# Turning the attention probabilities of a prompt in 64-query halves instead of 128-query tiles

## The reference, cut to what matters

```python
s_w = jnp.einsum('bqgpd,bwgd->bqgpw', qg, kw) - slope * d_w
p_w = masked_softmax(s_w, m_w)
o_w = jnp.einsum('bqgpw,bwgd->bqgpd', p_w, vw)
...
o = g[..., 0:1] * o_c + g[..., 1:2] * o_s + g[..., 2:3] * o_w
```

## Time and profile before

| | |
|---|---|
| median of 3 runs | 1911.8 us |
| lowest and highest | 1909.61, 1912.58 us |
| profiled execution: its span, first to last instruction | 1903.0 us (the page gives no other time of this execution) |
| TensorE matmuls busy | 1792.6 us, 94% |
| TensorE weight loads busy | 1441.7 us, 76% |
| VectorE busy | 672.6 us, 35% |
| ScalarE busy | 512.3 us, 27% |
| GpSimd busy | 100.0 us, 5% |
| chain that ended last | TensorE 47%, issue 8%, VectorE 5%, ScalarE 1% |
| prompt attention | from about 1310 to 1470 us |

### The profile page before, as it was taken

The page is one execution under the profiler, slowest core; times in us unless marked ns, Lnnn a source line. Parts: engine busy times, 40 slices in busy tenths (PEclk is TensorE's granted clock), DMA queues, the critical chain, the costliest instruction groups (busy, mean ns, idle before and its releaser), DMA issues.

```text
span 1903.0 us, 52710 instructions
## 1 busy us (share of the span) xinstructions
PE 1792.6 (94%) x23279; PEld 1441.7 (76%) x23279; DVE 672.6 (35%) x1804; ACT 512.3 (27%) x1216; POOL 100.0 (5%) x155
## 2 busy tenths in 40 slices
PE   6999999999898898999998999899999989999997
PEld 4876777777777577899987854687777778999985
DVE  6140226677664333111103400406887241111104
ACT  3112223333332122111112300315888131111103
POOL 2111100000000002000002000000000001000002
PEclk9999999999999898999999999999999998999998
DMA  8665835434434497999978992543000387999944
GB/s 308 213 213 193 269 115 169 119 111 123 120 108 146 130 274 270 387 409 415 418 314 252 223 220 90 169 111 103 2 2 2 77 346 268 411 413 417 417 179 169
DMA packets 195382, 413.48 MB, mean 217 GB/s; under 512 B 53686, under 2 KB 135314, under 8 KB 186674
## 3 DMA queue, kind: packets, MB, share of 16 engines
q1 hardware_dynamic: 176386, 357.95, 54.9%
q0 software_dynamic: 11040, 39.85, 5.8%
q10 hardware_dynamic: 7760, 12.79, 1.9%
HBM read 356.84 MB, written 57.91 MB: 218 GB/s over the span
## 4 chain that ended last, share of the span: by engine, by line
PE 47%; issue 8%; DVE 5%; ACT 1%; DVEq 1%; ACTq 0%
PE bank L2009 12%; PE bank L2004 6%; PE bank L2022 5%; PE bank L2028 4%; PE bank L1731 3%; PE bank L2888 3%; PE bank L2109 2%; PE bank L1986 1%; PE bank L1997 1%; PE bank L2998 1%; PE bank L3033 1%; DVE region_a L3299 1%; PE bank L2945 1%; PE bank L2820 1%; DVEq L3321 1%
## 5 line engine op out<-in xcount | busy, mean ns | idle before, releaser
L2004 PE MATMUL bank<-wg,slot_x 128*32 128x384 f32 x1056 | 123.0, 504 | 4.0 <-ACT slot_x L2198 2.7
L2009 PE MATMUL bank<-wg,slot_x 128*32 128x128 f32 x1056 | 124.4, 280 | 0.0
L2004 PE MATMUL bank<-wu,slot_x 128*32 128x384 f32 x1056 | 119.0, 486 | 3.7 <-issue 3.7
L2009 PE MATMUL bank<-wu,slot_x 128*32 128x128 f32 x1056 | 119.2, 273 | 0.0
L2022 PE MATMUL bank<-wd,actT 128*32 128x384 f32 x1056 | 117.5, 486 | 1.4 <-ACT actT L2221 1.4
L2028 PE MATMUL bank<-wd,actT 128*32 128x256 f32 (+1 forms) x704 | 118.1, 326 | 0.0
L2009 PEld LDWEIGHTS bank<-wg,slot_x 128*32 128x32 f32 x1056 | 116.7, 113 | 1.2
L2009 PEld LDWEIGHTS bank<-wu,slot_x 128*32 128x32 f32 x1056 | 115.2, 110 | 2.3
L639 PE MATMUL bank<-xm,wp 128*128 128x272 f32 x480 | 113.3, 395 | 0.0
L639 PEld LDWEIGHTS bank<-xm,wp 128*128 128x128 f32 x480 | 90.2, 190 | 20.7 <-issue 2.7
L2434 DVE TENSOR_TENSOR act<-bank,act 128x384 f32<-128x384 f32 x32 | 17.9, 558 | 249.0 <-PE bank L2009 249.0
(11 more groups left out here) (649 smaller groups left out, 4033.5 us busy)
## 6 DMA issues: line engine op xcount, KB each, us to landing
wg<-in_moe_w_gate_dram SPq DMA_DIRECT2D x22, 2048.0 KB, 11.6
wu<-in_moe_w_up_dram SPq DMA_DIRECT2D x22, 2048.0 KB, 16.3
wd<-in_moe_w_down_dram SPq DMA_DIRECT2D x22, 2048.0 KB, 11.6
xT<-in_ada_w_dram SPq DMA_DIRECT2D x40, 1024.0 KB, 5.5
w<-in_moe_w_gate_dram SPq DMA_DIRECT2D x10, 2048.0 KB, 11.6
fT<-in_moe_w_up_dram SPq DMA_DIRECT2D x10, 2048.0 KB, 16.2
gall<-in_moe_w_down_dram SPq DMA_DIRECT2D x10, 2048.0 KB, 11.3
wp<-in_rwkv_w_rkv_dram SPq DMA_DIRECT2D x24, 512.0 KB, 4.7
```

What stands on the lines that cost most here:

```text
L2004: mm = pe.matmul(ps[32 * j:32 * j + 32, 0:GW], x[:, k, 32 * j:32 * j + 32], w[:, k, 0:GW], start=k == 0, stop=k == KT - 1)
L2009: mm = pe.matmul(ps[96:128, q * 128:(q + 1) * 128], x[:, kk, 32 * q:32 * q + 32], w[:, kk, GW:FF], start=kk == 0, stop=kk == KT - 1)
```

## The change

The turn of a prompt unit is done in halves of 64 queries. For each head and key tile there are two transposes, one from partitions 0 to 63 and one from partitions 64 to 127, each against the matching quarter of the identity, with 64 moving columns. Half r of both heads goes to bank 4 + r. The waits for the two copies of the unit before are drawn together into one wait ahead of all transposes. pt_tr is posted by the last transpose of each half. ScalarE still makes two copies a unit, now one for each half with both heads, written to pieces of 64 columns of PT. The sample units' turn is as it was. PT's contents are the same.

```diff
--- before.py
+++ after.py
@@ -2991,12 +2991,15 @@
         if u >= NU:
             return sample_turn(u)
         j, i, br = UNITS[u]
+        if u >= 1:
+            pe.wait_ge(S("pt_ev"), 2 * u)
         for h in range(2):
-            if u >= 1:
-                pe.wait_ge(S("pt_ev"), 2 * u - 1 + h)
             for kt in range(i + 1):
-                mm = pe.transpose(bank[4 + h][:, kt * 128:(kt + 1) * 128], B.sc[u % NSC][:, h, kt * 128:(kt + 1) * 128], ident[:])
-            mm.then_inc(S("pt_tr"), 1)
+                at = (h * (i + 1) + kt) * 64
+                for r in range(2):
+                    mm = pe.transpose(bank[4 + r][:, at:at + 64], B.sc[u % NSC][hs(r), h, kt * 128:(kt + 1) * 128], ident[hs(r), hs(r)])
+                    if (h, kt) == (1, i):
+                        mm.then_inc(S("pt_tr"), 1)
 
     def sample_values(u):
         bq, gp = SUNITS[u - NU]
@@ -3130,11 +3133,13 @@
             j, i, br = UNITS[u] if u < NU else (None, None, None)
             if u >= NPT:
                 act.wait_ge(S("pv_mm"), u - NPT + 1)
-            for h in range(2):
-                n = i + 1 if u < NU else 4 - h
-                act.wait_ge(S("pt_tr"), 2 * u + h + 1)
-                act.activation(B.PT[u % NPT][:, h, 0:n], bank[4 + h][:, 0:128 * n].rearrange("p (k t) -> p k t", t=128), ACT.Copy)\
-                   .then_inc(S("pt_ev"), 1)
+            for r in range(2):
+                act.wait_ge(S("pt_tr"), 2 * u + r + 1)
+                if u < NU:
+                    dst, src = B.PT[u % NPT][:, :, 0:i + 1, r * 64:r * 64 + 64], bank[4 + r][:, 0:128 * (i + 1)].rearrange("p (h k t) -> p h k t", h=2, t=64)
+                else:
+                    dst, src = B.PT[u % NPT][:, r, 0:4 - r], bank[4 + r][:, 0:128 * (4 - r)].rearrange("p (k t) -> p k t", t=128)
+                act.activation(dst, src, ACT.Copy).then_inc(S("pt_ev"), 1)
             if (i, br) == (0, 0):
                 act.wait_ge(S("ptc_tr"), j + 1)
                 act.activation(B.PTc[j % 2], bank[6], ACT.Copy).then_inc(S("ptc_ev"), 1)
```

## The result

| | before | after |
|---|---|---|
| median (6 runs each) | 1910.7 us (1903.31 to 1915.73) | 1892.56 us (1888.32 to 1898.82) |
| ratio | | 0.9916, 95% interval 0.9893 to 0.9939 |
| span of the profiled execution | 1903.0 | 1890.1 |
| attention: first scores (line 2945) to the first matmul of the output projection (line 1731) | 183.61 | 177.51 |
| from there to the end | 415.52 | 408.87 |

The change makes the kernel faster by 18.1 us by these medians; later repetitions of both kernels put it at about 12. Forecast was 6.7. The attention gives 6.1 of the profiled difference of 12.9; 6.7 lie behind it and 0.15 ahead of it, where the change touches nothing.

A forecast was written before the change was run, and what follows sets the result against it. TensorE and VectorE were taken to share the bound in the prompt attention. Seven waits shortened by 0.79 (5.5 us) plus 1.2 at its end made 6.7 off 1911.8: 1905.1 us, range 1900.0 to 1914.0.

The forecast's parts named there:

- The bound: Prompt attention: TensorE and VectorE share the bound; VectorE's seven waits for scores shrink from 1.41 to 0.62 us each.
- behind the last compressed turn: End of the attention, after VectorE's last wait: TensorE sets the time, and shorter turns and passages save 1.2 us.
- the passage from turn to values: Prompt attention, last transpose to first values: 0.20 us instead of 0.11; the change of shape, 0.09, stays.
- The pairs side by side: Prompt turns: two half-height transposes run together, 0.06 us a pair, saving 0.05 of each 0.11.
- loads set the pace: Prompt turns: weight loads take 0.11 us a pair, so turns save nothing; 1910.6 us, chance 0.06.
- The second rival: Prompt turns: halves follow each other, with the relief of shape; 1915.0 us, chance 0.09.
- the passage from turn to scores: Prompt attention: the shared shape removes the 0.09 us change of shape and the exposed load, 0.20 together.
- The slower case: Prompt turns: halves follow each other and transposes don't share the scores' configuration, no passage gets cheaper; 1916.7 us, chance 0.10.
- the wait vanishes: Prompt attention: copies report sooner or the queue fills better, so the full 9.9 + 1.5 us go; 1900.4 us, chance 0.05.
- all later work moves with it: Behind the attention: output weights load when the values are done, so later work moves by the same 6.7 us.
- part on costs: Prompt attention on TensorE: 0.11 us a transpose step, 0.16 for the first, 0.09 for a change of shape.
- The base: Whole kernel: 6.7 us taken off the runs' median 1911.8, which lies 8.8 above the span of 1903.0.

The follow-up runs named there:

- The two kernels with the halves in turn: Kernel after, all transposes of queries 0 to 63 before those of 64 to 127: with a wait per half 0.9972, with one wait 1905.9 us.
- the single wait: Kernel after with all of half 0 transposed before half 1, and one wait for both copies ahead of all transposes: 1905.9 us.
- The shape break: Kernel after plus one full-shape (128*128), one-column matmul between the second turn of each pair of units and the scores: 1900.1 us.
- another order: Kernel after with second turn and following scores ahead of the second values once a head pair, ScalarE's store at its step's end: 0.9934 and 0.9948.
- the padding: 64 tiny transposes (128 TensorE instructions, results unused) ahead of the second layer's output projection: added to the kernel before 0.9997, to the kernel after 0.9966.

## Why the prediction was right in the attention and wrong in the time

**The bound was right.** VectorE's waits for the scores went from seven of 1.41 to eight of at most 0.62 and their sum to 4.4, "at 4 us in all" as predicted. From the second compressed turn on the attention gained 6.7 where 6.7 was summed, and 1.2 of it behind the last compressed turn as summed; a head pair gained 0.88 (one of the six 1.11) where 0.79 was summed. The starts of the turns hit to 0.05 us. That the values came at 0.64 and not 0.69 is the passage from turn to values: the prediction kept its 0.20 whole, but its 0.09 for the change of shape now come on top of 0.06 a pair, 0.15 in all.

**The pairs side by side** were priced rightly (0.06 a pair, 0.062 measured). The rival that loads set the pace at 0.11 is refuted by it. The Trainium skill's rule (TensorE: Matmul & The Clock Gate, "LDWEIGHTS") would give 0.11 too (an estimate, 128 columns at P/1.2 ns), and these rows don't agree with it. The second rival, halves one after another, is refuted as a mechanism by the 3 ns. Its price of 1915.0 was not tested: it supposed the pairs of the change, each 0.12 long, with both copies 1.32 us behind the turn's start. The two kernels with the halves in turn have half 0 complete early; with the single wait its copy starts at 3.43 (the rival: 4.19) and the third turn comes at 4.66 (5.40). What they show is that the order of the halves in the program gains 0.02 to 0.12 us a head pair of the 0.88. At least 0.20 of it is the passage from turn to scores; the rest was not taken apart.

**The slower case**, no shared configuration, was wrong on both of its conditions: the halves run side by side, and no idle time stands between turn and scores. The shape break, which adds a matmul of its own, gives an upper bound for the second condition: 3.7 us in the attention, which leaves 3.0 of the gain. That the wait vanishes did not happen either; 0.6 stayed, and it took another order to halve it.

**What failed** is the step "so all later work moves with it", by which the difference was taken one to one. The later work did not merely move. The prediction's part on costs counted what each added instruction takes on TensorE's array and gave no line to their number in the program: 640 more of them shift the code behind, and a stop of 2.5 us that the kernel before has at line 2004, and that stands in its trace, goes away; in two of the four traces that have it the clock falls behind it. It is worth 2.4 to 5.6 us, 4.0 on the mean of the four. With the 6.7 of the attention that makes 10.7 of a measured 12.3 +- 1.9. The other 1.6 us are unexplained and within the scatter. That the place of the code decides the stop is shown by the padding; that the fetch of a block is what TensorE stands for is argued from the packet in flight, not shown.

**The base** was off too. The prediction put 8.8 us between span and median down to what is around the span. The profiled execution after has 1.75 us around it (1891.85 less 1890.1). The rest was that the profiled execution of before was one of the faster ones: such executions differ above all by how long the granted clock is at 0.50 when the experts start (from 705 to 760 us it is 0.88 in this execution and 0.72 in its repetition, whose span is 9.2 us longer). And 1911.8 is 3.1 above the mean of all runs of the unchanged kernel, 1908.7. Against that mean the same sum gives 1902.0. So of the 12.5 us between forecast and result 3.1 are the base and 3.8 a favourable set of six runs (1892.56 against 1896.4 over all). The other 5.6 are the step above: 4.0 for the stop on the mean of its traces, 1.6 open. None of it is in the attention.

The range reached down to 1900.0 for a wait that vanishes; no case in it had a gain outside the attention. The chain's share of 8% "issue" said that the engine also stands for causes that the profile doesn't name. A case in which the added instructions move such a stop, by 2.4 to 5.6 us, was missing. That the attention came out right to 0.1 us is in part luck: each of six head pairs gained 0.09 to 0.32 more than summed, and the seventh, the first in time, gained nothing that shows: the attention's first 26 us are 25.97 before and 26.08 after on the mean of the traces.

## What to carry to other kernels

Where a partial-height operation borders on another, give both the same tile shape first; the order in which its halves are issued mattered less here, since the halves overlap either way. Where a kernel has loops and some 50,000 instructions, look behind each loop for an idle time with no releaser, since an edit that adds instructions ahead of it can remove or create it: price it separately, and try padding before you ascribe the difference to the edit. Compare stages between fixed instructions, behind the point where the clock has settled, not spans, when executions scatter more than the change is worth.

## What the runs showed of the hardware that was not expected

- Leaving the long loop, TensorE can stand for 2.0 to 2.7 us, with an instruction packet in flight; 128 idle instructions added ahead make the stop come or go. The fall of the clock behind it (0.50, then 1.00 by 1819.6 in the padded kernel) comes on top in some executions.
- Transposes of 64 rows in the two halves of the array start 3 ns apart. The Trainium skill (TensorEngine Tiling (Array Packing), "Key Properties") says that a change between tile modes needs a drain; the passage from 64\*128 to 128\*64 stayed as it was, 0.09 us above the rate of the turn (1363.26 less 1362.62 is 0.64 us, with the last pair 0.49 after the first: 0.15 instead of 0.06 for a step), and the passage from turn to scores, 64\*128 on both sides, has none. The difference agrees with that rule.
- Neighbouring groups of one tile shape ran into each other here. With the halves in turn, the second half starts 0.305 us into the turn and the first half's last transpose at 0.485. Scores of one half start before the last transposes of the other half, and the turn and the compressed scores of the kernel after interleave. Its TensorE timeline at a head pair's start:

```profile
1357.75 0.27 PE L3000 MATMUL bank<-ident,region_a 64*128 64x64 f32 x1
1357.85 0.27 PE L2966 MATMUL bank<-kcT,region_a 64*128 64x31 f32 x1
1357.86 0.27 PE L3000 MATMUL bank<-ident,region_a 64*128 64x64 f32 x1
1357.96 0.27 PE L2966 MATMUL bank<-kcT,region_a 64*128 64x31 f32 x1
```

- With the halves in turn the granted clock fell to 0.50 for 3.4 us inside the attention, behind its first 20 us, six times in two traces, and in none of the other eleven; what sets it off is open.
